# Two result copies moved ahead, one broadcast product moved behind, and filler matmuls added, at the entrance of a transformer block's up projection

## The reference

```python
x = x + merged @ w_out[l]
x = x + conv_ffn(rmsnorm(x, ffn_norm_g[l]), w_up[l], conv_w[l], conv_b[l], w_down[l])

def conv_ffn(h, w_up, conv_w, conv_b, w_down):
    gu = h @ w_up
    gate, up = gu[..., :D_FF], gu[..., D_FF:]      # D_FF = 2816 = 22 * 128
    gate = lax.conv_general_dilated(gate, ...) + conv_b     # causal, 3 taps, each column by itself
    return (gelu(gate) * up) @ w_down
```

## Time and profile before

| what | value |
|---|---|
| median of 3 runs | 2549.83 us (2549.59 to 2551.64) |
| profiled execution, its own time | 2548.3 us |
| its span | 2546.5 us |
| PE busy | 2474.3 us, 97% of the span |
| DVE busy | 1514.4 us, 59% |
| ACT, POOL busy | 868.2 us and 754.7 us |

### The profile page before, as it was taken

One profiled execution on the slowest core, in us unless ns is written; L12 is line 12 of the kernel. 1 busy time (PEld: TensorE's weight loads), 2 busy tenths in 40 slices (PEclk: granted clock), 3 DMA queues, 4 the chain that ended last, 5 costly groups with the idle time before them and its releaser, 6 DMA issues.

```text
span 2546.5 us, 33485 instructions
## 1 busy us (share of the span) xinstructions
PE 2474.3 (97%) x12202; PEld 2045.7 (80%) x12202; DVE 1514.4 (59%) x1983; ACT 868.2 (34%) x1291; POOL 754.7 (30%) x442
## 2 busy tenths in 40 slices
PE   8999999999999999999999999999999999999998
PEld 5777787787887888888888878788888888788886
DVE  7856674835557877777421573377777764633354
ACT  4232222222224544444100232156666651222121
POOL 3232232332333655555344412200000003222221
PEclk9999999999999999999999999999999999999999
DMA  5134343421433223233544211100000001111112
GB/s 182 42 118 139 100 149 116 140 68 51 164 107 108 100 105 126 99 108 135 227 179 142 83 44 36 56 1 18 8 8 8 9 9 61 40 34 33 41 41 74
DMA packets 54418, 210.71 MB, mean 83 GB/s; under 512 B 6420, under 2 KB 7700, under 8 KB 49082
## 3 DMA queue, kind: packets, MB, share of 16 engines
q1 hardware_dynamic: 50340, 194.92, 22.4%
q10 hardware_dynamic: 3990, 14.59, 1.6%
HBM read 173.30 MB, written 38.55 MB: 83 GB/s over the span
## 4 chain that ended last, share of the span: by engine, by line
PE 84%; DVE 11%; issue 3%; ACT 2%; DMA 0%; DVEq 0%; ACTq 0%; SPq 0%
PE PS L733 38%; PE PS L1044 16%; PE PS L1073 9%; PE PS L1329 4%; PE PS L1262 3%; PE PS L1268 3%; PE PS L1301 2%; PE PS L903 1%; PE PS L938 1%; DVE cols L2863 1%; PE PS L1252 1%; DVE SC L2393 1%; PE PS L784 1%; PE PS L773 1%; PE PS L1483 1%
## 5 line engine op out<-in xcount | busy, mean ns | idle before, releaser
L733 PE MATMUL PS<-H,w_hl 128*128 128x512 f32 x4368 | 1027.6, 394 | 15.4 <-DVE H L2204 3.8
L733 PEld LDWEIGHTS PS<-H,w_hl 128*128 128x128 f32 x4368 | 814.4, 188 | 204.6 <-issue 22.3
L682 POOL CAST w_hl<-w_raw 128x1024 fp32r<-128x1024 f32 x138 | 154.7, 1121 | 1538.1 <-PE PS L733 959.9
L684 POOL TENSOR_TENSOR w_hl<-w_raw,w_hl 128x1024 fp32r<-128x1024 f32 x138 | 347.5, 2518 | 11.0
L1044 PE MATMUL PS<-BT,WS 128*128 128x512 f32 x1056 | 247.2, 390 | 0.6 <-issue 0.6
L1073 PE MATMUL PS<-FFD,w_hl 128*128 128x512 f32 x1056 | 239.8, 389 | 0.1
L1044 PEld LDWEIGHTS PS<-BT,WS 128*128 128x128 f32 x1056 | 198.2, 188 | 42.5 <-issue 1.5
L1073 PEld LDWEIGHTS PS<-FFD,w_hl 128*128 128x128 f32 x1056 | 198.1, 188 | 41.6 <-DVEq L2516 0.5
L1044 PE MATMUL PS<-B,WS 128*128 128x512 f32 x792 | 189.5, 393 | 2.5 <-issue 2.5
L1044 PEld LDWEIGHTS PS<-B,WS 128*128 128x128 f32 x792 | 150.2, 190 | 34.4 <-issue 3.1
L689 POOL TENSOR_TENSOR WS<-w_raw,WS 128x512 fp32r<-128x512 f32 x88 | 140.2, 1602 | 73.0 <-ACT WS L1804 72.7
(11 more groups left out here) (350 smaller groups left out, 3101.5 us busy)
## 6 DMA issues: line engine op xcount, KB each, us to landing
w_raw<-in_units SPq DMA_DIRECT2D x186, 512.0 KB, 3.6
AW<-in_ada SPq DMA_DIRECT2D x48, 512.0 KB, 4.3
ff_part<-FFS SPq DMA_DIRECT2D x20, 1024.0 KB, 4.9
FFD<-ff_part SPq DMA_DIRECT2D x20, 1024.0 KB, 5.8
X<-in_x SPq DMA_DIRECT2D x8, 512.0 KB, 8.1
x_part<-SC SPq DMA_DIRECT2D x8, 512.0 KB, 2.6
X<-x_part SPq DMA_DIRECT2D x4, 1024.0 KB, 8.7
out<-X SPq DMA_DIRECT2D x16, 256.0 KB, 2.1
```

The lines of the kernel that those rows point to most:

```text
L682: pool.tensor_copy(hi_part, raw).then_inc(w_hi, 1)
L684: pool.tensor_tensor(lo_part, raw, hi_part.bitcast(F32), ALU.subtract).then_inc(w_split, 1)
L733: mm = pe.matmul(PS[:, out_at + a:out_at + a + m], w(s, wp, w0 + k), src[:, o:o + m], start=(k == 0 and wp == 0 and xp == 0), stop=(k == k ...
```

## The change

Three edits, all of them for the first pair only:

```diff
-        def norm_sum(idx, p2, parts=((ACC, T),), early=None, warm=None):
+        def norm_sum(idx, p2, parts=((ACC, T),), early=None, warm=None, fill_at=0, fill=0):
...
             for late in (False, True):
+                if late and fill:
+                    busy(fill, fill_at)
                 if late or early is None:
...
                         if warm and seen in warm:
-                            busy(1, 0)
+                            busy(1, fill_at)
...
                 if first and n == 1:
-                    norm_sum(before("norm2", "norm"), before("norm2", 2), early=before("norm2", "square") - 1)
-                elif first and n == 3:
+                    norm_sum(before("norm2", "norm"), before("norm2", 2), early=before("norm2", "square") - 1,
+                             warm=(4, 12), fill_at=2560, fill=5)
+                elif first and n == 5:
                     norm_spread(before("norm2", "norm"), before("norm2", 3))
...
             b_at, c_at, a_at = SUM_AT[q]
-            snap(p, 1, FIRST[q], b_at)
-            high_parts(0, 1)
             if isinstance(p, int) and p == 0:
+                high_parts(0, 1)
                 act.wait_ge(lo, before("out1", "split") + operand_at(4, HK - 1) + 1)
-            if spilled:
-                act.wait_ge(ff_out, p * 16 - 16)
-            snap(p, 2, KEEP[q][:, HALF:T], c_at)
+                chain(act.activation(KEEP[q][:, HALF:T], FIRST[1], ACT.Copy))
+            else:
+                snap(p, 1, FIRST[q], b_at)
+                high_parts(0, 1)
+                if spilled:
+                    act.wait_ge(ff_out, p * 16 - 16)
+                snap(p, 2, KEEP[q][:, HALF:T], c_at)
...
         high_part(0, 3, 0)
+        act.wait_ge(x_out, 16 * KC)
+        act.wait_ge(sq_ready, before("norm2", "square"))
+        for n in range(2):
+            snap(0, n + 1, FIRST[n], SUM_AT[0][n])
         late_hi(0, (T2_SUMS[1], T2_SUMS[3]))
...
         act.wait_ge(done[2], before("norm2", 2) + 1)
-        act.wait_ge(x_out, 16 * KC)
         up_pair(0, 0, spilled=False)
```

## The result

The changed kernel took 2554.95 us (median of 20 runs), the one before 2551.47 us (20 runs). The ratio is 1.0015, 95% interval 1.0008 to 1.0021: about 3.8 us or 0.15% slower, between 2 and 5.4 us (the two medians by themselves differ by 3.5 us). The forecast was 4.0 us on top of a median of 2549.83 us, 2553.8 us in all, with a range of 2550.6 to 2556.3; here the kernel before took 1.6 us more than in the three runs that the forecast started from, so the total came out 1.1 us higher although the change cost slightly less. The profiled execution has a span of 2555.0 us, which is 8.5 over the one before; only a part of that belongs to the change, as the next paragraphs show.

The account below looks back on a forecast made before the run. PE was taken as the bound almost everywhere, with product 5 held by DVE's line 2680. Broadcast 1.7 plus clock 2.3 gave +4.0 us on a median of 2549.8: 2553.8 us, range 2550.6 to 2556.3.

Parts of the forecast that it names:

- The door: At the entrance, product 5 waits for DVE's first addition (line 2680), which ends at 823.73 us and stays there.
- Early copies and fillers at nothing: Around products 2 and 3: PE's earlier waits go, but product 5 still waits for DVE; cost and gain nothing.
- The broadcast in the unbroken run: Behind product 5, where PE runs without pause, nothing hides the moved broadcast: +1.7 us (1.4 to 2.0).
- The clock: PE idles 8.2 us before product 5, its clock falls to half, and later work runs slowly: +2.3 us (0 to 3.4).
- No second wait: DVE's line 2688 comes 3.1 us later, but the second pair's room of 1.6 us becomes 2.5: no further wait.
- The sum: Whole kernel: 1.7 for the broadcast plus 2.3 for the clock, +4.0 us, 0.16% longer.
- The clock did not hold: Rival, pause before product 5: clock holds or is back at once, only the broadcast's +1.7 left, 2551.5 us; chance 0.17.
- DVE did not come sooner: Rival, DVE's list: line 2680 comes up to some 4 us sooner, at best 2547.5 to 2549.8 us; chance 0.06.
- nothing in its list before the door was set by PE: Rival, DVE's list: something taken as fixed was set by PE, time freed is gained, 2546.5 to 2549 us; chance 0.08.
- The long low stretch: Rival, after the pause: low clock wholly on needed work, or another wait; +5.1 to +7, 2555 to 2557 us; chance 0.22.
- the third case: The rival of low clock wholly on needed work or another wait following, +5.1 to +7 us; chance 0.22.
- the upper edge: The part of the main forecast over 0.2% slower, above 2554.9 us; counted with the third case in 0.22.

Follow-up runs that it names:

- the broadcast back: The changed kernel with the norm's broadcast again between products 3 and 4, early copies and fillers kept; 1.0003 of the kernel before (0.9994 to 1.0012).
- the door only: The kernel before with only DVE's list reordered, its first addition ahead of reciprocal, diagonals and BT3's low part; 1.0002 of the kernel before (0.9992 to 1.0011).
- the earlier door: The changed kernel with DVE's first addition moved ahead of reciprocal, diagonals and BT3's low part, first pair only; 0.9985 of the kernel before (0.9976 to 0.9994).

## Why the prediction was right

*The door.* Shown: DVE's first addition starts 24.35 to 24.41 us after product 0 in all seven profiles in which DVE's order is the old one. Product 5 follows it at 25.21 to 25.25 us in six of them, with late and early copies, with and without fillers. It moves by 6.1 us when DVE's order is changed and nothing else. In two kernels PE itself came later than the door: product 5 at 27.1 us with the broadcast back and at 26.1 with the door only.

*Early copies and fillers at nothing.* As a gain this holds: product 5 stands at 25.25 us without the fillers and at 25.21 without either. But the two edits are not free. The clock term below exists because PE now has one long pause, and with the broadcast moved it is the early copies that bring that pause (32.50 against 33.92 us). That 33.92 without fillers and 33.90 with them agree so closely is luck, since the changed kernel itself gave 33.90 and 35.39.

*The broadcast in the unbroken run, +1.7 us (1.4 to 2.0).* It measured 1.83 with a full clock throughout, and 1.76 when moved alone.

*The clock, +2.3 us (0 to 3.4).* It measured 1.3 and 2.8 in two profiles of the same program. The pause was 8.29 us (8.2 forecast) and the fall came in it, as taken. The size was a middle between bounds and not derived: that it fits is partly luck. The bounds went by low stretches of 3.4 and 6.8 us. The second profile had one of 10.2 us, and stayed under 3.4 us of loss because 4.1 us of it lay in the pause.

*No second wait.* Shown: DVE's reader of the broadcast started at 831.75 and PE had no pause from the second pair to the down projection.

*The sum.* 1.83 + 1.3 = 3.2 us in the first profile and 1.83 + 2.8 = 4.7 in the second, about 3.9 between them; the runs say 3.8 (2 to 5.4). The changed kernel and its repetition agree (1.0015 and 1.0016). So close an agreement says less than it seems, as the interval is 3.4 us wide. The forecast took 0.2% as the least change that can be told from none; with 20 runs of each kernel 0.15% could be told, as the whole interval lies above 1.

*The rivals.* The time excludes +1.7 us only just, and doesn't exclude +5.1; it is the traces that decide. The clock did not hold. DVE did not come sooner, and nothing in its list before the door was set by PE: the first addition kept its place to 0.06 us while PE's order changed. The long low stretch did occur, in the second profile (5.46 us for product 5, nearly twice its length), but not wholly on work, and even then the entrance lost 4.7 us. The chances of the outcomes had a slip: the third case alone has 0.22, so the upper edge that was to be in the same 0.22 had no share.

*The later expectations.* They missed in more places than the forecast, each time on a wait or a fall of the clock ahead of the door. With the earlier door I priced product 6 by its operand and forgot the copy that it also waits for (`st_snap`), which stood on ACT behind two high parts that DVE released late. With the broadcast back, product 5 was put at 25.2 us and came at 27.1. With the broadcast alone moved, a pause of 5 us was expected and 0.54 measured. With the door only, product 5 and the second pair came 0.7 us late.

## What to carry to other kernels

A wait is worth removing only if nothing later on the same engine's list waits for something that stays where it is. Here earlier copies and fillers brought PE earlier to a door that another engine opens, which gained nothing, and gathered its waits into one long pause in which the clock fell, which cost 1.3 to 2.8 us. The edit that moved work behind that door had its full price, 1.8 us. Moving the door itself by 6 us, with the same instructions in another order, turned the same edits into a gain. Where waiting can't be avoided, work that is needed anyway is best left inside the wait, where it is free. Whether it also keeps the clock up depends on the pause that is left: with pauses of 2.45, 0.63 and 0.60 us the clock was full from 813.2 us on in the kernel before, and with one of 5.64 us it fell.

## What was not expected of the hardware

The low stretch of the clock, in the same place of the same program and after the same pause of 8.3 us, lasted 6.8 us in one profile and 10.2 in the other, and after a pause of 5.6 us it lasted 3.4 us in one kernel and 6.8 in another. So the loss differs from one execution to the next by as much as its forecast size; how it is distributed, two profiles don't show.

Product 0 starts at 798.69 to 801.67 us in the ten profiles, though all ten programs are the same up to there. A difference of a few microseconds between two spans says little about a change of this size; the length of the stretch that the change touches says much more.
